# A one-core encoder layer: stages that end without waiting for their last stores, and the Fourier stage's sine unit loaded and folded one stage earlier

## The chip, the cores and the metric

The kernel runs on one core of one Trainium2 chip. The metric is the device time of one execution in microseconds (us); lower is better. The engines are named as in the profile: PE (TensorE, matrix multiplication), PEld (its weight loads), DVE (VectorE), ACT (ScalarE), POOL (GpSimd) and SP (SyncE, which only issues transfers here). SP's transfers go through one hardware queue (q1), POOL's through a software queue (q0), and both are served by the same 16 DMA engines.

## The reference, cut to what matters

Two sequences, of 512 and 2048 tokens with 1024 channels each, go through the same layer. The code works on their 2560 tokens together.

```
x    = layer_norm(x)
proj = x @ w_in                       # 1024 -> 1280: 512 Fourier, 512 q, 128 k, 128 v
f    = real(fft2(u, over tokens and the 128 channels of each of 4 groups)) @ w_fourier
a    = windowed attention (+-128 tokens, ALiBi, sink), 8 query heads, 2 key/value heads
x    = layer_norm(alpha * x + concat(f, a) @ w_out)
h    = square(relu(x @ w_ff1))        # 1024 -> 4096
x    = layer_norm(alpha * x + h @ w_ff2)
```

The answer has to be close to float32, so each large product is three matmuls: both operands are split into a rounded high part and a rest (`split_mm`, lines 65 to 67). ACT makes the high part and DVE the rest.

## The kernel before, in words

The program is six stages, one after the other, each in a block of its own. A block ends for all engines together: the next one starts when every engine, SP among them, has come to the end of its list. Between stages the data lie in DRAM.

- Stage a, `embed_project`: five groups of 512 tokens. In each group DVE normalises, PE transposes, and PE then makes ten units of 128 output rows (`UNITS`): 0 to 3 are queries, 4 keys, 5 values, 6 and 7 the cosine half of the Fourier channels, 8 and 9 the sine half. ACT takes unit m from PSUM into one of four slots of `stage`, and SP stores it to `proj` (line 228); a slot may be filled again when its last store has landed (`stage_st`). DVE also forms sums of the feed-forward weights, which SP loads and stores (lines 192 to 211). In the last group (`more` false) SP loads the DFT tables (line 2272) into what are later the keys' tiles, and, after unit 2, the short sequence's Fourier rows (`load_short_unit`, lines 2266 and 2268). DVE splits three of the five tables and folds the short unit (`fold_short`, line 525).
- Stage b, `fourier`: the transform along the tokens is made of seven units in a fixed order: short, sine0, sine1, left_short, left, cosine0, cosine1. For each, DVE adds or subtracts mirrored halves of the sequence (`fold`, lines 670 and 675), PE transposes the result (`turn`, line 862), ACT and DVE split it (`z_high`, line 767; `z_low`, line 687), and PE multiplies it with the tables in an even part and an odd part (`sums`). Two more tables are split here (`table_high`, line 759; `table_low`, line 681). Then the channel mixing (`mix_short`, `mix_long`) and five stores to `heads` (lines 644 and 649).
- Stage c, `attend`: the attention, 20 blocks of 128 tokens, each stored to `heads` (line 1067).
- Stage d, `mix_out`: the output projection, residual and norm, 20 tiles of 128 tokens. It stores `x1` (line 1378) and, for each pair of tiles, the operands and sums that the next product wants, 1792 KB in `xb` (lines 1382 and 1386).
- Stage u, `mlp_up`: the first feed-forward product in a seven-product scheme. It starts with weight sums that SP loads (line 1627), activations that were loaded during stage d (`x_first`) and four more slices that POOL loads from `xb` at its start (line 1686). Matmuls whose result nobody reads (`keep_busy`, line 73) fill PE's wait at the start of stages c, d, u and e.
- Stage e, `mlp_down`: the second feed-forward product, by far the longest; the change doesn't touch it.

What sets the order around the change: each engine works its own list in order, and waits on semaphores. SP's list holds nearly all transfers, so an SP instruction that waits holds back every transfer behind it. Four stages end with SP waiting for its own last stores: lines 258 and 259 (stage a), 650 and 651 (b), 1069 and 1070 (c), 1387 to 1389 (d).

Of the kernel before, what the change touches and what calls it, by code (L numbers as in the profile page):

```python
# [14 lines left out]
P = 128  # L15
D = 1024
# [88 lines left out]
def embed_project(nc, held, x, ln_g, ln_b, w_in, ident, ident_d, xn_d, proj_d, w2_d, t_d, w1_d, ws_d, k_raw, place, load_mixing,  # L105
                  load_short_unit, load_table, short_parts):
# [6 lines left out]
    with ExitStack() as ctx:  # L113
# [35 lines left out]
        stage_st = al.sems("stage_st", 4)  # L149
# [4 lines left out]
        first_tables, u_short, u_short_ld, t_raw_ld, (half_fold, ends, bias) = short_parts  # L154
        tables_split = al.sem("tables_split")
        PLAIN = FROW - FC

# [10 lines left out]
        def _(sp):  # L168
# [44 lines left out]
            def body(g, more):  # L213
# [3 lines left out]
                if more:  # L217
                    load_quad(g, 0)
                    load_quad(g, 1)
                else:  # L220
                    for i in range(3):
                        load_table(sp, i)
                    load_up(0)
                    load_up(1)
                for m in (1, 0, *range(2, UNITS)):
                    if m:
                        sp.wait_ge(stage_done, g * UNITS + UNITS + m + 1)
                    sp.dma_start(proj_d[m * P:(m + 1) * P, bass.ds(g * GRP, GRP)], stage[:, m % 4, :]
                                 ).then_inc(stage_st[m % 4], 16)
                    if not more and m == 2:  # L230
                        for slot in range(4):
                            sp.wait_ge(stage_st[slot], uses(slot) * 16 + 16)
# [6 lines left out]
                    if more and m in (5, UNITS - 1):  # L239
                        for j in (0, 1) if m == 5 else (2, 3):  # L240
                            store_sums(g, j)
                    if not more and m == 5:
                        store_up(0)
                        store_up(1)
                    if more and m == 5:
                        load_quad(g, 2)
                        load_quad(g, 3)
# [3 lines left out]
            with sp.Fori(0, NG - 1) as g:  # L251
                body(g, True)
# [5 lines left out]
            for s in range(4):  # L258
                sp.wait_ge(stage_st[s], 16 * (uses(s) * NG + 1))
# [32 lines left out]
        def _(dve):  # L292
# [115 lines left out]
            for i, (raw, hi, lo) in enumerate(first_tables):  # L408
# [7 lines left out]
                if i == 1:  # L416
                    dve.wait_ge(u_short_ld, 48)
                    fold_short(dve, u_short, half_fold, ends, bias)

        @block.scalar  # L420
        def _(act):
# [19 lines left out]
            def body(g, first):  # L441
# [12 lines left out]
                for m in range(UNITS):  # L454
                    act.wait_ge(proj_done, g * UNITS + m + 1)
                    act.wait_ge(stage_st[m % 4], g * (16 * uses(m % 4)) + (m // 4) * 16 + 16)
                    is_q = m < KROW // P
                    act.mul(stage[:, m % 4, :], bank[:, m % 8, :], QSCALE if is_q else 1.0
# [6 lines left out]
        def _(pe):  # L465
# [3 lines left out]
            def body(g, first):  # L469
# [17 lines left out]
                for m in range(UNITS):  # L487
                    out = bank[:, m % 8, :]
                    if m >= 8:
                        pe.wait_ge(stage_done, g * UNITS + UNITS + m - 7)  # L490
                    for k in range(KT):
# [4 lines left out]
                        if m == 0:  # L496
# [28 lines left out]
def fold_short(dve, u_short, half_fold, ends, bias):  # L525
# [10 lines left out]
    for kind in range(2):  # L536
        for tiles, op in parts:
            op = op if kind == 0 else {ALU.add: ALU.subtract, ALU.subtract: ALU.add}[op]
            dve.tensor_tensor(to[:, kind, tiles, :], halves[:, 0, tiles, :], halves[:, 1, tiles, :], op)


def fourier(nc, held, proj_d, mixing, ident, u_short, short_table, tables, raw_tables, t_ld, folding, heads_d, load_keys_values,
            load_queries):
# [20 lines left out]
    with ExitStack() as ctx:  # L564
# [5 lines left out]
        heads_more = [al.sb(f"heads{i}", [P, LONG]) for i in range(2)]  # L570
# [6 lines left out]
        mix = al.sb("mix", [P, NFG, 2, P])  # L577
        bank = al.ps("bank", [P, 8, 512])

        u_cos0, u_flat = u_short, u_short.rearrange("p i t -> p (i t)")  # L580
        place = [u_flat, u_a[:], u_b[:], u_left[:, LONG:], u_left[:, 0:LONG], u_flat, u_a[:]]
        out = [heads_more[0][:], heads_more[1][:], u_b[:], u_left[:, 0:LONG], heads_more[0][:]]
# [10 lines left out]
        out_st = al.sems("out_st", 5)  # L593
        block = al.block()

        def folds(n):

            return place[n][:, 0:2 * (ODD0 if units[n] == "left_short" else 512)].rearrange("p (k s) -> p k s", k=2)
# [13 lines left out]
        def _(sp):  # L612
# [17 lines left out]
            load_sines(0, u_a, u_ld[1])  # L630
# [4 lines left out]
            sp.wait_ge(turned, 2 * 0 + 2)  # L635
            sp.dma_start(u_flat, rows(0, P, tok)).then_inc(u_ld[5], 16)
            sp.wait_ge(turned, 2 * 1 + 2)
            sp.dma_start(u_a[:], rows(P, P, tok)).then_inc(u_ld[6], 16)
# [11 lines left out]
            for slot in range(5):  # L650
# [3 lines left out]
        def _(pool):  # L654
            pool.memset(u_left[:], 0.0).then_inc(left_zero, 1)
            pool.memset(y_short[:, :, WIDE0:EVEN0], 0.0).then_inc(y_zero, 1)
            pool.wait_ge(turned, 2 * 5 + 2)
# [4 lines left out]
        def _(dve):  # L662
# [63 lines left out]
            def mirrored_long(g):  # L726
# [3 lines left out]
                if g == 3:  # L730
# [8 lines left out]
            fold(1)  # L739
            z_low(1)  # L740
            table_low(0)
# [14 lines left out]
        def _(act):  # L756
# [12 lines left out]
            def copy_mix():  # L769
                for i in range(2):  # L770
# [51 lines left out]
            def straight_long(g):  # L822
# [3 lines left out]
                if g == 3:  # L826
# [7 lines left out]
            table_high(0)  # L834
            table_high(1)
            z_high(1)
# [16 lines left out]
        def _(pe):  # L853
            def turn(n):
# [3 lines left out]
                for kind in range(2):  # L858
                    if n:
                        pe.wait_ge(fold_done, 2 * (n - 1) + kind + 1)  # L860
# [1540 lines left out]
```

## Time and profile before

| | us |
|---|---|
| median of 3 runs | 2475.83 (2475.64 to 2476.02) |
| the profiled execution's own time | 2474.14 |
| its span | 2472.4 |
| PE busy | 2377.8 (96%) |
| DVE busy | 1578.8 (64%) |
| ACT busy | 1089.9 (44%) |
| DMA moved | 547.76 MB, 222 GB/s |

The span runs from the first to the last recorded instruction; the execution's own time is 1.74 us more. A busy engine is one with an instruction on it; PE's matmuls overlap, so that its busy time is no measure of its peak. Where a row says "[3.50 <-PEq L113]", the engine had been idle for 3.50 us, and what ended that was the event at line 113. PEq, SPq and DVEq are the engines' sequencers, which also carry the block ends; an event of a sequencer at line 113, 564, 967, 1337 or 1564 is the change from one stage to the next.

### The profile page before, as it was taken

The numbers are of one execution on the slowest core, as the hardware profiler recorded it, in microseconds if no ns is written. First come the engines' busy times: TensorE is split into PE (matmuls) and PEld (weight loads), VectorE is DVE, ScalarE is ACT, GpSimd is POOL, SyncE is SP. The second block draws the span as 40 slices with busy tenths as digits, with TensorE's granted clock in tenths as the row PEclk, the third lists the DMA queues.
The fourth block names the chain that finished last, engine by engine and source line by source line (L and its number), as shares of the span: only waits on it lengthen the run. The fifth ranks groups of instructions, "written<-read, shape, count | busy, mean of one in ns | idle before, by whom it ended". The sixth has DMA issues, their size and how long they took to land. (4 is left out here: it accounts for less than half of the span.)

```text
span 2472.4 us, 35019 instructions
## 1 busy us (share of the span) xinstructions
PE 2377.8 (96%) x12038; PEld 2072.4 (84%) x12038; DVE 1578.8 (64%) x2218; ACT 1089.9 (44%) x1770; POOL 181.6 (7%) x245
## 2 busy tenths in 40 slices
PE   6999978999999979999999999999999999999998
PEld 5888866999788858888899989998888888888886
DVE  8644455766566676666766676666455586668667
ACT  3111135888311144444555555555433344444442
POOL 1000001222122210000000000000000010001001
PEclk9999989999999989999999999999999999999999
DMA  7766755223255855555766676668866668777974
GB/s 274 286 270 231 281 164 212 78 72 93 90 196 199 298 238 209 210 214 196 277 240 243 244 278 242 244 230 290 278 195 193 188 216 326 228 219 252 308 226 135
DMA packets 220153, 547.76 MB, mean 222 GB/s; under 512 B 21640, under 2 KB 90888, under 8 KB 200332
## 3 DMA queue, kind: packets, MB, share of 16 engines
q1 hardware_dynamic: 203968, 488.19, 56.8%
q0 software_dynamic: 16080, 58.20, 7.3%
q8 instruction: 62, 1.02, 0.2%
q14 instruction: 43, 0.35, 0.0%
HBM read 365.95 MB, written 180.36 MB: 221 GB/s over the span
## 5 line engine op out<-in xcount | busy, mean ns | idle before, releaser
L65 PE MATMUL e_bank<-e_hi,e_lo 128*128 128x512 f32 x1120 | 435.8, 389 | 0.6 <-DVE e_lo L2112 0.6
L66 PE MATMUL e_bank<-e_lo,e_hi 128*128 128x512 f32 x1120 | 435.7, 389 | 0.0
L67 PE MATMUL e_bank<-e_hi 128*128 128x512 f32 x1120 | 435.7, 389 | 0.0
L65 PE MATMUL u_bank<-u_x_hi,u_wa_lo 128*128 128x384 f32 (+1 forms) x768 | 271.7, 354 | 2.7 <-ACT c_vt_raw L1845 1.4
L67 PE MATMUL u_bank<-u_x_hi,u_wa_hi 128*128 128x384 f32 (+1 forms) x768 | 271.0, 353 | 0.0
L2112 DVE TENSOR_TENSOR e_lo<-e_raw,e_hi 128x896 fp32r<-128x896 f32 (+1 forms) x168 | 189.3, 1134 | 120.6 <-ACT e_hi L2083 119.8
L2083 ACT CAST e_hi<-e_raw 128x896 fp32r<-128x896 f32 (+1 forms) x168 | 165.2, 983 | 209.3 <-PE e_bank L67 199.1
L65 PEld LDWEIGHTS e_bank<-e_hi,e_lo 128*128 128x128 f32 x1120 | 210.2, 188 | 45.1 <-DVE e_lo L2112 1.4
L66 PEld LDWEIGHTS e_bank<-e_lo,e_hi 128*128 128x128 f32 x1120 | 210.2, 188 | 43.7
L67 PEld LDWEIGHTS e_bank<-e_hi 128*128 128x128 f32 x1120 | 210.2, 188 | 43.5
L65 PE MATMUL u_bank<-u_x_hi,u_wb_lo 128*128 128x384 f32 (+1 forms) x576 | 204.9, 356 | 9.2 <-DVE u_x_rest L1694 9.2
L67 PE MATMUL u_bank<-u_x_hi,u_wb_hi 128*128 128x384 f32 (+1 forms) x576 | 204.3, 355 | 0.0
L66 PE MATMUL u_bank<-u_x_rest,u_wb_hi 128*128 128x384 f32 (+1 forms) x576 | 204.3, 355 | 0.0
L66 PE MATMUL u_bank<-u_x_first,u_wa_hi 128*128 128x384 f32 (+1 forms) x576 | 203.4, 353 | 0.0
L65 PEld LDWEIGHTS u_bank<-u_x_hi,u_wa_lo 128*128 128x128 f32 x768 | 144.6, 188 | 15.8 <-issue 2.7
L65 PE MATMUL a_bank<-a_xt_hi,a_w_lo 128*128 128x512 f32 x400 | 156.8, 392 | 0.6 <-DVE a_xt_lo L361 0.6
L66 PE MATMUL a_bank<-a_xt_lo,a_w_hi 128*128 128x512 f32 x400 | 156.2, 391 | 0.0
L67 PE MATMUL a_bank<-a_xt_hi,a_w_hi 128*128 128x512 f32 x400 | 156.1, 390 | 0.0
L67 PEld LDWEIGHTS u_bank<-u_x_hi,u_wa_hi 128*128 128x128 f32 x768 | 144.4, 188 | 10.0
L2112 DVE TENSOR_TENSOR e_lo<-c_q_raw,e_hi 128x896 fp32r<-128x896 f32 (+1 forms) x84 | 94.8, 1134 | 66.8 <-ACT e_hi L2083 66.8
L2112 DVE TENSOR_TENSOR e_lo<-c_vt_raw,e_hi 128x896 fp32r<-128x896 f32 (+1 forms) x84 | 94.9, 1134 | 61.4 <-ACT e_hi L2083 57.9
L1120 DVE CUSTOM_DVE_ANT_0 c_prob<-c_sc,c_bias,c_neg_sink 128x384 f32<-128x384 f32 (+1 forms) x160 | 93.8, 589 | 62.4 <-PE c_sc L1220 44.0
(273 smaller groups left out, 4527.2 us busy)
## 6 DMA issues: line engine op xcount, KB each, us to landing
u_w_sum<-s_ws SPq DMA_DIRECT2D x34, 1024.0 KB, 4.8
c_vt_raw<-w_ff SPq DMA_DIRECT2D x24, 1024.0 KB, 7.8
c_q_raw<-w_ff SPq DMA_DIRECT2D x24, 1024.0 KB, 8.0
s_h<-c_k_raw SPq DMA_DIRECT2D x32, 768.0 KB, 7.2
e_raw<-s_t SPq DMA_DIRECT2D x96, 256.0 KB, 3.7
e_raw<-s_h SPq DMA_DIRECT2D x112, 192.0 KB, 2.8
ab_place<-w_ff SPq DMA_DIRECT2D x18, 1024.0 KB, 8.5
s_h<-c_k_raw SPq DMA_DIRECT2D x96, 192.0 KB, 2.4
```

What stands on the lines that cost most here:

```text
L65: tensor.matmul(out, w_lo, m_hi, start=first, stop=False, skip_group_check=again)
L66: tensor.matmul(out, w_hi, m_lo, start=False, stop=False, skip_group_check=again)
L67: return tensor.matmul(out, w_hi, m_hi, start=False, stop=last, skip_group_check=again)
L1120: dve.tensor_tensor_reduce(prob[:, h % 4, 0:w], sc[:, h % 2, 0:w], bias[:, h, kbs[0] * P:kbs[0] * P + w], 1.0, neg_sink[:, h:h + 1], ALU.a ...
L2083: act.copy(part(hi, n), part(raw, n)).then_inc(hi_done, 1)
L2112: dve.tensor_tensor(part(lo, n), part(raw, n), part(hi, n).bitcast(F32), ALU.subtract).then_inc(split, 1)
```

## The change

Four stages no longer end with the wait for all their last stores. The semaphores of those stores live on into the next stage, and whoever reads the data, or writes over the tile that is being stored, waits there.

The order of the units in stage a changes for every group but the first: 8, 9, 6, 7, 0 to 5. In the last group the short unit is loaded first, ahead of the tables; the sums of `w_ff1` are stored after the fourth unit, tables 3 and 4 are loaded after the fifth and the eighth unit, and after the sixth SP waits for the short unit's fold and loads unit sine0 (`load_sine_unit`), which DVE folds at the end of its list (`fold_sine`). In stage b that fold is gone, and z_high(1) stands ahead of table_high(1), table_low(0) ahead of z_low(1).

```diff
 # embed_project
+        def order(first):
+            sines = FROW // P + 2
+            return list(range(UNITS)) if first else [sines, sines + 1, *range(FROW // P, sines), *range(FROW // P)]
 # SP, last group ahead of the units
+                    load_short_unit(sp)
                     for i in range(3):
                         load_table(sp, i)
                     load_up(0)
                     load_up(1)
-                for m in (1, 0, *range(2, UNITS)):
+                for i in (1, 0, *range(2, UNITS)):
...
-                    if not more and m == 2:
...
-                        load_short_unit(sp)
-                    if not more and m in (6, UNITS - 1):
-                        i = 3 if m == 6 else 4
-                        sp.wait_ge(tables_split, i - 1)
-                        load_table(sp, i)
+                    if not more and i == 3:
+                        store_up(0)
+                        store_up(1)
+                    if not more and i in (4, 7):
+                        table = 3 if i == 4 else 4
+                        sp.wait_ge(tables_split, table - 1)
+                        load_table(sp, table)
+                    if not more and i == 5:
+                        sp.wait_ge(stage_st[0], 16 * (uses(0) * (NG - 1) + 2))
+                        sp.wait_ge(short_folded, 1)
+                        load_sine_unit(sp)
...
-            for s in range(4):
-                sp.wait_ge(stage_st[s], 16 * (uses(s) * NG + 1))
 # DVE, end of the stage
+            dve.wait_ge(u_sine_ld, 64)
+            fold_sine(dve, u_sine, half_fold, sine_folds)
 # new
+def fold_sine(dve, u, half_fold, to):
+    q = SEQS[1][1] // 4
+    low, high = u
+    dve.drain()
+    dve.tensor_tensor(half_fold[:, 0, :], low[:, 1:q + 1], high[:, 2 * q - 1:q - 1:-1], ALU.subtract)
+    dve.tensor_tensor(half_fold[:, 1, :], low[:, 2 * q - 1:q - 1:-1], high[:, 1:q + 1], ALU.subtract)
+    dve.drain()
+    for kind in range(2):
+        dve.tensor_tensor(to[:, kind, :], half_fold[:, 0, :], half_fold[:, 1, :], ALU.add if kind else ALU.subtract)
+        def load_sine_unit(sp):     # 4 transfers of 64 x 1024, 256 KB each
+            for half in range(2):
+                for part in range(2):
+                    tok = SEQS[1][0] + part * 1024
+                    sp.dma_start(u_sine[part][half * HD:(half + 1) * HD, :], ...).then_inc(u_sine_ld, 16)
 # fourier, SP
-            load_sines(0, u_a, u_ld[1])
+            for slot in range(4):
+                sp.wait_ge(stage_st[slot], stores(slot) - 32)
             load_sines(1, u_b, u_ld[2])
...
+            sp.dma_start(u_a[:], rows(P, P, tok)).then_inc(u_ld[6], 16)
+            sp.wait_ge(turned, 2 * 1 + 2)
             sp.dma_start(u_flat, rows(0, P, tok)).then_inc(u_ld[5], 16)
+            for slot in range(4):
+                sp.wait_ge(stage_st[slot], stores(slot))
...
-            for slot in range(5):
+            for slot in range(4):
                 sp.wait_ge(out_st[slot], 16)
 # fourier, POOL ahead of the queries and ACT in copy_mix: wait for stage_st of all slots
 # fourier, DVE and ACT: the order of the first steps
             z_low(0)
-            fold(1)
+            table_low(0)
             z_low(1)
-            table_low(0)
             table_low(1)
...
             z_high(0)
             table_high(0)
+            z_high(1)
             table_high(1)
-            z_high(1)
 # attend, SP
-            for s in range(2):
-                sp.wait_ge(ot_st[s], 16 * (NB // 2))
 # attend: POOL waits for the last Fourier store ahead of load_first_heads, DVE ahead of its first normalise
+            pool.wait_ge(fourier_st, 16)
 # mix_out, SP
-                sp.wait_ge(mixed_st[s], 16 * (NT // 4))
+            sp.wait_ge(mixed_st[0], 16 * (NT // 4))
 # mix_out: POOL ahead of its first load and DVE in norm(0) wait for ot_st of both slots
 # mlp_up, ACT ahead of x_high(0, 2), POOL ahead of the last group
+            act.wait_ge(xb_st, 16 * (NT // 4))
```

Some tiles move, so that what is still being stored isn't written over: `heads_more` behind `mix` (and the last two Fourier outputs into it), `mixed` to the end of `place`, `neg_sink` ahead of `nmax`.

## Rows read from the trace of the kernel before

**Rows 1.** The page: engine's busy time, share of the span, instructions.
```profile
PE 2377.8 (96%) x12038; PEld 2072.4 (84%) x12038; DVE 1578.8 (64%) x2218; ACT 1089.9 (44%) x1770; POOL 181.6 (7%) x245
```
**Rows 2.** PE's waits, whole span: in total, times, longest (us).
```profile
PE u_bank L73 <- PEq L1337: 11.7, 1, 11.7
...
PE b_bank L862 <- PEq L113: 3.5, 1, 3.5
...
PE c_sc L1219 <- DVE c_qs L1112: 1.8, 1, 1.8
```
**Rows 3.** SP's waits, whole span.
```profile
SPq L1389 <- DMA s_xb<-d_place: 5.5, 1, 5.5
...
SPq L651 <- DMA s_heads<-b_heads: 3.4, 1, 3.4
...
SPq L1070 <- DMA s_heads<-c_ot: 1.9, 1, 1.9
...
SPq L259 <- DMA s_proj<-a_stage: 1.3, 1, 1.3
```
**Rows 4.** SP in order of time: start, us, instruction; the stage ends.
```profile
318.84 0.33 SPq L228 DMA_DIRECT2D s_proj<-a_stage  x1
...
321.64 1.18 SPq L621 DMA_DIRECT2D b_u_a<-s_proj  x2
...
400.43 0.33 SPq L649 DMA_DIRECT2D s_heads<-b_u_left  x1
...
408.17 0.34 SPq L1061 DMA_DIRECT2D c_bias<-bias  x1
...
883.69 0.32 SPq L1382 DMA_DIRECT2D s_xb<-d_place  x1
887.71 0.32 SPq L1386 DMA_DIRECT2D s_xb<-d_place  x1
894.03 15.49 SPq L1627 DMA_DIRECT2D u_w_sum<-s_ws  x2
```
**Rows 5.** PE at the one change of stage without such a wait (u to e).
```profile
1696.56 1.95 PE L73 MATMUL e_bank<-c_k_raw 128*128 128x512 f32 x4 [0.30 <-PEq L1564]
```
**Rows 6.** Stage b's start, all engines in order of time.
```profile
324.02 3.81 ACT L759 CAST b_t_last<-c_k_raw 128x2112 fp32r<-128x2112 f32 x2
...
329.82 1.29 DVE L670 TENSOR_TENSOR b_folding<-b_u_a 128x512 f32<-128x512 f32 x2 [4.97 <-DMA b_u_a<-s_proj]
...
332.03 1.94 PE L862 MATMUL b_bank<-ac_ident,b_u_a 128*128 128x128 f32 x8 [5.15 <-DVE b_u_a L675]
...
334.00 0.58 ACT L767 CAST b_z_hi<-b_bank 128x512 fp32r<-128x512 f32 x1 [0.27 <-PE b_bank L862]
...
335.23 4.62 DVE L681 TENSOR_TENSOR b_t_last<-c_k_raw,b_t_last 128x2112 fp32r<-128x2112 f32 x2
```
**Rows 7.** Windows: PE, PEld, DVE, ACT, POOL busy (count), granted clock, DMA.
```profile
321.60:326.90 5.30, 4.64 (x20) 4.08 (x20) 1.38 (x2) 3.94 (x4) 2.31 (x2) 0.52 1.03 300
...
417.70:420.00 2.30, 1.75 (x10) 1.32 (x10) 1.24 (x5) 1.06 (x4) 1.35 (x2) 1.00 1.02 417
```
**Rows 8.** DVE in the last group of stage a.
```profile
301.30 1.43 DVE L532 TENSOR_TENSOR b_folding<-c_q_raw 128x256 f32<-128x256 f32 x4
...
307.44 1.26 DVE L413 CAST b_table<-c_k_raw 128x2112 fp32r<-128x2112 f32 x1 [2.80 <-issue]
```
**Rows 9.** Issues of 269 to 297 us: KB each, median us to landing.
```profile
c_q_raw<-s_proj SPq DMA_DIRECT2D x1, 512.0 KB, 14.8
```
**Rows 10.** Issues of 403 to 420 us, and DVE's first need of the bias.
```profile
c_bias<-bias SPq DMA_DIRECT2D x1, 1536.0 KB, 7.0
...
416.37 1.22 DVE L1112 TENSOR_TENSOR c_qs<-c_q_raw,c_qs 64x1024 fp32r<-64x1024 f32 x1 [0.17 <-issue]
```
**Rows 11.** Stage u's start: ACT's wait for the sums, and the issues of 888 to 925 us.
```profile
898.91 1.05 ACT L1812 CAST u_wa_hi<-u_w_sum 128x1024 fp32r<-128x1024 f32 x1 [0.20 <-DMA u_w_sum<-s_ws]
...
u_x_rest<-s_xb POOLq DMA_DIRECT2D x4, 1024.0 KB, 10.4
```

More of the change, by code:

```diff
@@ L417, in _ @@
                     dve.wait_ge(u_short_ld, 48)
-                    fold_short(dve, u_short, half_fold, ends, bias)
+                    fold_short(dve, u_short, half_fold, ends, bias).then_inc(short_folded, 1)
+            dve.wait_ge(u_sine_ld, 64)
+            fold_sine(dve, u_sine, half_fold, sine_folds)
         @block.scalar
@@ L453, in body @@
                             w_high_rest(k + early)
-                for m in range(UNITS):
-                    act.wait_ge(proj_done, g * UNITS + m + 1)
-                    act.wait_ge(stage_st[m % 4], g * (16 * uses(m % 4)) + (m // 4) * 16 + 16)
+                for i, m in enumerate(order(first)):
+                    act.wait_ge(proj_done, g * UNITS + i + 1)
+                    act.wait_ge(stage_st[i % 4], g * (16 * uses(i % 4)) + (i // 4) * 16 + 16)
                     is_q = m < KROW // P
-                    act.mul(stage[:, m % 4, :], bank[:, m % 8, :], QSCALE if is_q else 1.0
+                    act.mul(stage[:, i % 4, :], bank[:, i % 8, :], QSCALE if is_q else 1.0
                             ).then_inc(stage_done, 1)
@@ L486, in body @@
                         mm.then_inc(turned, 1)
[L487 to L490, printed above, removed]
+                for i, m in enumerate(order(first)):
+                    out = bank[:, i % 8, :]
+                    if i >= 8:
+                        pe.wait_ge(stage_done, g * UNITS + UNITS + i - 7)
                     for k in range(KT):
@@ L649, in _ @@
                 sp.dma_start(heads_d[g * P:(g + 1) * P, tok], out[1 + g]).then_inc(out_st[1 + g], 16)
-            for slot in range(5):
+            for slot in range(4):
                 sp.wait_ge(out_st[slot], 16)
@@ L656, in _ @@
             pool.memset(y_short[:, :, WIDE0:EVEN0], 0.0).then_inc(y_zero, 1)
+            for slot in range(4):
+                pool.wait_ge(stage_st[slot], stores(slot))
             pool.wait_ge(turned, 2 * 5 + 2)
@@ L769, in copy_mix @@
             def copy_mix():
+                for slot in range(4):
+                    act.wait_ge(stage_st[slot], stores(slot))
                 for i in range(2):
@@ L1410, in _ @@
             pool.wait_ge(const_set, 2)
+            for s in range(2):
+                pool.wait_ge(ot_st[s], 16 * (NT // 2))
             for n in range(NT):
@@ L1467, in norm @@
                 dve.wait_ge(mix_done, n + 1)
+                if n == 0:
+                    for slot in range(2):
+                        dve.wait_ge(ot_st[slot], 16 * (NT // 2))
                 dve.wait_ge(xn_ld[s], 16 * (n // 2 + 1))
@@ L1552, in _, with mlp_up @@
             transpose(NT - 1)
[L1555 removed]
+def mlp_up(nc, held, xb_d, w1_d, ws_d, h_d, first, xb_st, h_st, h_sum_st, load_down):
     NP = FF // (2 * P)
```

109 lines of the change are left out of this document (62 added, 47 removed).

## The prediction

> **What bounds the kernel now.** I read the page first: PE has an instruction on it for 96% of the span [rows 1], so time can go only where PE stands still or where its clock is low. Then PE's waits in total: the reader is to see that the longest single ones end in a sequencer event at a change of stage, 11.7 us ahead of stage u and 3.5 ahead of stage b [rows 2], and that others stand inside the start of stage b. Then SP's waits: four of them, 1.3, 3.4, 1.9 and 5.5 us, are the waits for a stage's own last stores [rows 3], and SP in order of time shows that the next stage's first issue follows each at once [rows 4]. So the four ends of stages are bound by the landing of stores, and stage b's start by a load and its fold: PE waits 5.15 us there for the fold of unit sine0 [rows 6]. Nothing else in the change lies on a path that PE waits for.
>
> **What a block end costs by itself.** At the end of stage d SP's last issue ends at 887.71 + 0.32 = 888.03, its wait at 893.53, and the next issue stands at 894.03 [rows 3, 4]: 0.5 us for the change itself. At the one change that has no such wait PE is idle 0.30 us only [rows 5]. I take 0.5 for each.
>
> **1. Stage a to b.** Before, the last store is issued by 319.17, and stage b's SP begins at 321.64 [rows 4]. Between them lie the issue of table 4, the 1.3 us wait and 0.5. After, table 4 is issued earlier in the group and the wait is gone: b begins at 319.17 + 0.5 = 319.7, **1.9 us earlier**. The sine unit's read in b of `stage_st` asks for stores that landed several units before. The cost end: nothing if DVE is done by then, which is the cover to be checked in step 5.
>
> **2. Stage b's start.** The load of sine0 and its fold leave stage b (four DVE instructions, two pairs of 1.29 us), and turn(1) no longer waits for them. What is late next? PE is free for turn(1) at 332.03 - 5.15 = 326.88, thus 325.0 with step 1's shift. From the start of turn(1) to the end of the second z_high it is 334.58 - 332.03 = 2.55 us: 327.5. Now table_high(1) stands behind it, half of 3.81 = 1.9: 329.4. Then table_low(1), half of 4.62 = 2.3: 331.7 [rows 6]. Before, the two table_low ended at 339.85 [rows 6]. Everything of stage b behind that hangs on DVE's order: take_cosines_short, fold(2), turn(2). Its other inputs (u_b, now the first load of the stage; the left rows; the tables) are issued as early or earlier. So **8.1 us** if PE runs as it did, 6.2 of them inside b.
>
> PE's clock adds to it. In 321.6 to 326.9 the granted clock was 0.52, half, after PE's idle time at the change; in 417.7 to 420.0, right behind an idle time of 1.8 us, it was 1.00 [rows 2, 7]. After the change the idle time ahead of stage b falls to 3.5 - 1.9 = 1.6 us, nearest to the second row. At full clock the 4.64 us of PE's work ahead of turn(1) and the turn itself halve; with the latencies between PE, ACT and DVE I count 1.2 us off up to turn(1) and 0.9 in it, **2.1 us** in all, since each ACT step that follows starts that much earlier. I take it, as an estimate from these rows; the ends are 0 and 2.6. Steps 1 and 2: 1.9 + 6.2 + 2.1 = **10.2 us**, ends 8.1 and 10.7.
>
> The added waits in b (POOL ahead of the queries, ACT in copy_mix, SP ahead of the keys) ask for the stores of stage a's last group, issued by 319.17, and are reached 20 us or more later: nothing. The output tiles trade places, and the third output now waits for the short store, more than 10 us old by then: nothing.
>
> **3. Stage b to c.** SP's wait was 3.4 us; it began at 408.17 - 0.5 - 3.4 = 404.27. A store of a group takes 0.33 + 3.4 = 3.7 us; the third group's, issued at 400.43, landed at 404.1 [rows 3, 4]. So without the last one the wait is over when it begins: **3.4 us** off. Against it: the bias (1536 KB) is now issued while that last store still holds the queue. It took 7.0 us to land from 408.17, thus 415.2, and DVE came to it at 416.37 [rows 10]: 1.2 us of cover. The remaining 3.4 us of store less some 1 us of start-up that can overlap takes up to 2.4 of it. Cost between 0 and 1.2, I take 0.2, since the last part of a landing is latency in which the bias already moves. **3.2 us**, ends 2.2 and 3.4.
>
> **4. Stage c to d.** The 1.9 us wait goes [rows 3]. ACT's and DVE's first work there reads what landed in stage c; the loads that need the last stores come 2.9 us into the stage, and the stores are in by then. **1.9 us**, ends 1.6 and 1.9.
>
> **5. Stage d to u.** SP now waits for the last but one `xb` store only. The last took 0.32 + 5.5 = 5.8 us [rows 3, 4]; the one of 883.69 therefore landed at 889.5, and stage u begins at about 890.0 instead of 894.03: 4.0 us earlier. But what paces the start of u is ACT's L1812 at 898.91, which waited for the weight sums, 0.20 us [rows 11]; they landed 4.9 us after their issue. Now the sums (1 MB) are issued on SP's queue behind a store of 1792 KB that lands at 893.5, so that its data end near 892.9. One MB at 417 GB/s, the rate of a full window [rows 7], is 2.5 us, a landing adds about 0.6, and POOL's four loads of 1 MB [rows 11], also 4 us earlier, take a share of the engines from about 894 on, which I put at 1 us. So the sums land at 892.9 + 2.5 + 0.6 + 1.0 = 897.0 against 898.9: **1.9 us**. Ends: 4.0 if the sums were not held at all, and below nothing, -1.8, if POOL's loads take half from their issue on (2.1 MB of SP's queue and as much of POOL's from 890.6 at 417 GB/s is 10.1 us, 900.7). Past this ACT and DVE work back to back until PE's wait for `u_x_rest`, so the shift stays.
> The Trainium skill ("DMA: Bandwidth & Descriptors", Queues, rings and completion order) says that each DMA engine takes turns between the queue rows that have work, a packet at a time. By it the sums share from the moment that POOL's descriptors are there; counted from the issue it would give the end of -1.8 and a total of 13.5 us, which is the rival on the sums below. That the wait of 0.20 us stood so small before is no proof of the rule or against it.
>
> **6. The last group of stage a.** This is what the moved work costs. The short unit (1 MB) now runs ahead of the tables and of `w_ff1`: at 300 to 417 GB/s [rows 7] DVE's sums are 2.5 to 3.5 us later, so fold_short begins at 301.30 + 2.8 = 304.1 [rows 8] and ends 3.3 us later, 307.4. SP stands at its wait for it, with the stores of units 6 to 9 and table 4 behind; ACT needs their slots only at 312.9 and 318.2, PE needs no bank of them: nothing. The sine unit's four issues end near 309.9 (0.59 each [rows 4]). DVE splits table 2 meanwhile, 307.4 to 311.2. Before, sine0 needed 8.2 us from its issue to the fold with a table ahead of it [rows 4, 6]; with table 3 ahead that gives 315.7, and the fold (2.7 us) ends at 318.4. DVE would be done 0.8 us ahead of SP's last issue. Cost 0; each us later costs one.
>
> **Sum.** 10.2 + 3.2 + 1.9 + 1.9 = 17.2 us. The profiled execution took 2474.14, so 2456.9 by its own time; the median of the runs shown is 1.7 us above it. Predicted: **2458.6 us**.
>
> **Rivals.**
> - Clock low at stage b's start. For: so it was in the rows, and in this start PE works in short bursts. Against: the idle time is halved. Total 15.1, 2460.7 us. Chance 0.22.
> - The sums of stage u land late, by taking turns with POOL's loads. For: both queues are served at once. Against: before, both began together as well, and the sums still landed in 4.9 us. Total 17.2 - 1.9 - 1.8 = 13.5, 2462.3 us. Chance 0.12.
> - The waits go but the next stage is held by something else (a code load, the engines' own start), 1 us at each of four changes. Against: the 0.30 us of stage e [rows 5]. 13.2, 2462.6 us. Chance 0.05.
> - The sine unit's fold ends stage a. For: the short unit once took 14.8 us to land [rows 9]; by that from 309.9 the fold ends at 327.4, 8.2 late, total 9.0, 2466.8 us. Against: the queue is nearly empty by 308. Chance 0.04.
> - The other side, slower: the same place, SP's list in order. If the wait for quad sums, table split and short fold grows so that the sine unit's landing comes two such times after its issue, 309.9 + 29.6, the fold ends at 342.2, stage b begins at 342.7 instead of 319.7, and the total is 23.0 - 17.2 = 5.8 us slower, 2481.6. It decides from a fold that ends after 336.4. Chance 0.03.
> - The change doesn't do what it says: a new wait in the readers (ACT ahead of x_high(0, 2), DVE in its first norm) stands for the same landing. Against: each is reached after it by the rows. Within 0.2%, 2474. Chance 0.04.
>
> **How the numbers follow.** The forecast has 0.50. Its own ends: -1.5 (clock partly low), -1.0 (bias), -1.0 (sums), +2.1 (sums not held), so 2456 to 2461.5. The range takes in the first three rivals: 2454.5 to 2464.5. What a measurement can tell from no change is 0.2%, 5 us: faster by more than that holds for the forecast and the first four rivals, 0.93; within it 0.04; slower 0.03.
>
> **What would show it.** After: SP's waits at the four ends gone, or under 0.5 us; PE's idle time ahead of b near 1.6 us; turn(1) right behind the short unit's sums, granted clock 1.00 in b's first 3 us (else the first rival); the two table_low end about 10 us after b's start, against 18; no DMA wait of DVE or PE behind table 2's split at the end of stage a, and DVE done before SP; ACT's L1812 waiting 2 to 3 us for the sums in u. Wrong: PE idle more than 2 us at a change with a DMA behind it, DVE's fold_sine later than SP's last store, or stage c's first bias add later than its matmul.

## The result, and the profile after the change

| | before | after |
|---|---|---|
| median, us | 2475.93 (2475.64 to 2476.51, 4 runs) | 2461.31 (2460.95 to 2461.50, 4 runs) |
| the profiled execution, us | 2474.14 | 2461.47 |
| its span, us | 2472.4 | 2459.8 |
| PE busy, us | 2377.8 | 2373.9 |

The ratio is 0.9943, with a 95% interval of 0.9931 to 0.9954: 14.6 us faster. Forecast were 2458.6 us and 17.2 us off, so some 2.7 us too much. The two profiled executions differ by 12.7 only. The last matmul of stage a starts at 317.80 before and at 319.72 after. In the eleven runs below it stands between 317.58 and 319.60, so this is scatter of stage a (after the change PE's first wait, for a load at the start, took 13.9 us against 12.7, and the granted clock was 0.83 in the first 40 us against 1.00), and the sums are made from stage to stage.

SP's waits for the stores of the stage that ends (in total, times, longest, us). The first is the only one left at a stage's end, where there were four, of 5.5, 3.4, 1.9 and 1.3 us [rows 3]; the second is the new reader's wait at the start of stage b:

```profile
SPq L1423 <- DMA s_xb<-d_place: 1.2, 1, 1.2
...
SPq L650 <- DMA s_proj<-a_stage: 0.2, 1, 0.2
```

PE's waits for a change of stage, and the one for stage c's first queries:

```profile
PE u_bank L73 <- PEq L1372: 7.4, 1, 7.4
PE c_sc L1254 <- DVE c_qs L1145: 4.6, 1, 4.6
...
PE c_pt L1288 <- PEq L588: 1.7, 1, 1.7
PE b_bank L896 <- PEq L113: 1.7, 1, 1.7
PE d_turn L73 <- PEq L1001: 1.5, 1, 1.5
```

They were 11.7 ahead of u and 3.5 ahead of b [rows 2]. The end of stage a and the start of b, in order of time (start, us, instruction), DVE and then PE:

```profile
317.83 0.69 DVE L559 TENSOR_TENSOR b_folding<-c_q_raw,c_vt_raw 128x512 f32<-128x512 f32 x1 [4.46 <-DMA c_vt_raw<-s_proj]
...
319.20 1.29 DVE L563 TENSOR_TENSOR c_q_raw<-b_folding 128x512 f32<-128x512 f32 x2
...
330.31 2.36 DVE L714 TENSOR_TENSOR b_t_last<-c_k_raw,b_t_last 128x2112 fp32r<-128x2112 f32 x1 [1.16 <-ACT b_t_last L791]
```
```profile
319.72 0.39 PE L67 MATMUL a_bank<-a_xt_hi,a_w_hi 128*128 128x512 f32 x1
...
321.84 1.07 PE L896 MATMUL b_bank<-ac_ident,c_q_raw 128*128 128x128 f32 x8 [1.73 <-PEq L113]
...
325.88 1.93 PE L896 MATMUL b_bank<-ac_ident,c_q_raw 128*128 128x128 f32 x8
...
337.81 1.94 PE L896 MATMUL b_bank<-ac_ident,b_u_b 128*128 128x128 f32 x8 [4.09 <-DVE b_u_b L708]
```

The reader is to see that turn(1), at 325.88, waits for nothing (before 5.15 us, [rows 6]), that the second table_low ends at 332.67, 10.8 us behind the stage's start, and that DVE's fold ends stage a at 320.49, behind PE's last matmul but ahead of SP's last issue (321.16). But turn(1) takes 1.93 us, which is its time at half clock; the first turn, with the same eight instructions, took 1.07. Windows of stages b and c (columns as in [rows 7]; the granted clock is the third number from the end):

```profile
321.80:324.50 2.70, 1.70 (x14) 1.49 (x14) 1.29 (x2) 2.00 (x3) 2.19 (x2) 1.00 0.74 216
324.60:327.80 3.20, 3.20 (x18) 3.20 (x17) 2.34 (x2) 1.41 (x2) 0.03 (x1) 0.50 0.93 202
328.00:334.00 6.00, 4.44 (x35) 4.03 (x34) 4.75 (x7) 3.65 (x6) 0.00 (x0) 1.00 0.88 347
356.10:361.40 5.30, 5.30 (x25) 5.30 (x26) 2.21 (x7) 1.36 (x4) 0.00 (x0) 0.50 0.39 162
408.40:412.00 3.60, 3.19 (x12) 2.64 (x13) 1.82 (x8) 1.58 (x6) 1.35 (x2) 0.50 1.03 422
```

TensorE was granted full clock (2.4 GHz) at the start of b, then half (1.2 GHz) for 3.4 us, and half again around the wait of 4.09 us ahead of turn(2) (from 334.8 to 341.6) and where it had just stood still for 3.04 us (at 356) and for 4.56 us (at 408). Stage u's start, SP, ACT and the issue with its landing (KB, median us to landing):

```profile
876.84 0.32 SPq L1420 DMA_DIRECT2D s_xb<-d_place  x1
878.88 0.34 SPq L1666 DMA_DIRECT2D u_w_sum<-s_ws  x1
```
```profile
886.37 1.05 ACT L1853 CAST u_wa_hi<-u_w_sum 128x1024 fp32r<-128x1024 f32 x1 [2.82 <-DMA u_w_sum<-s_ws]
```
```profile
s_xb<-d_place SPq DMA_DIRECT2D x1, 1792.0 KB, 6.9
u_w_sum<-s_ws SPq DMA_DIRECT2D x1, 1024.0 KB, 7.5
```

The sums needed 4.9 us before and ACT waited 0.20 for them [rows 11]. The two traces from piece to piece, all by PE's starts (turn(2) is the MATMUL L896 on b_u_b; "4th wait of u" is the wait of PE for DVE's x_low of 1.14 us that ends at 918.88 before and at 906.37 after):

| piece | before | after | gain | predicted |
|---|---|---|---|---|
| last matmul of a to first of b | 3.88 | 2.12 | 1.8 | 1.9 |
| b's start to turn(2) | 23.30 | 15.97 | 7.3 | 8.3 |
| turn(2) to b's last matmul | 57.08 | 58.40 | -1.3 | 0 |
| b's last to c's first | 6.13 | 2.76 | 3.4 | 3.2 |
| c's first to c's last | 222.75 | 223.09 | -0.3 | 0 |
| c's last to d's first | 4.14 | 2.16 | 2.0 | 1.9 |
| d's last to 4th wait of u | 37.90 | 36.26 | 1.6 | 1.9 |
| sum | | | 14.4 | 17.2 |

### The profile page after: what moved, and what is told of

Same layout as the page of the kernel before. It is cut to its first block and busy times, and to the rows that moved or that the text cites. A ratio compares the mean times of both kernels' runs of the same rounds, so it can differ in the third digit from the quotient of the medians.

```text
span 2459.8 us, 35018 instructions
## 1 busy us (share of the span) xinstructions
PE 2373.9 (97%) x12038; PEld 2071.2 (84%) x12038; DVE 1579.1 (64%) x2218; ACT 1089.4 (44%) x1770; POOL 180.7 (7%) x245
```

## The experiments

Eleven runs, of ten kernels, were made beside the kernel before, on three chips, where its medians were 2475.27, 2475.94 and 2476.72. The theory: the stores' waits and the sine unit's load are worth what the prediction says, and the 2.7 us that are lacking are TensorE's clock (2.6 us in the second, third and fifth rows of the table). Each kernel is the changed one with the edit shown. Medians are compared with the changed kernel's 2461.31, with the ratio to the kernel before of the same chip beside it. From the 4th wait of u to the end, which no edit reaches, the traces took between 1553.4 and 1558.0 us (1553.5 before, 1553.4 after), so a difference of 1 or 2 us is read from the stages and not from the medians.

**The four waits put back** (one of four alike shown):

```diff
             for j in range(TPG):
                 sp.wait_ge(xn_st[j], 16 * (NG + 1))
+            for s in range(4):
+                sp.wait_ge(stage_st[s], 16 * (uses(s) * NG + 1))
```

> The changed kernel with the four waits of SP for a stage's own last stores put back; the sine unit stays in stage a. Theory (the waits stand on the path that PE waits for, each worth what the comparison of the two traces gave: a to b 1.8, b to c 3.4, c to d 2.0, d to u 1.65 us): 8.8 us slower than the changed kernel, so about 2470.1 us, and PE's idle time ahead of stages b and u back at 3.5 and 11.7 us. First rival (another wait, such as the start of the engines or the code, holds the next stage anyway): under 5 us slower, and PE's idle time at the changes grows by less than SP's waits. Second rival (stage b's start is slowed by the clock as well when the idle time ahead of it is 3.5 us): 10 to 11 us slower, with the granted clock at half from b's first instruction.

Measured: 2469.16 us (2467.24 to 2471.18, 9 runs), ratio 0.9971 (0.9961 to 0.9981), 7.8 us slower. PE's waits for a change of stage:

```profile
PE u_bank L73 <- PEq L1376: 11.1, 1, 11.1
PE c_pt L1292 <- PEq L590: 5.2, 1, 5.2
PE d_turn L73 <- PEq L1003: 3.5, 1, 3.5
PE b_bank L898 <- PEq L113: 3.4, 1, 3.4
```

By pieces, against the changed kernel: a to b 1.7 us longer, b to c 3.4, c to d 2.0, d to the 4th wait of u 1.7; that is 8.8, as expected. Stage b inside was 0.5 us quicker and stage c 0.9, which leaves 7.4. At the end of d the wait moved stage u's start by 4.3 us (13.1 us behind the start of d's last matmuls against 8.8), but the time by 1.7 only. In stage c the clock is the likely reason: PE began it at half clock after 5.2 us of idle time, its keep-busy matmuls there took longer, the idle time ahead of the scores was 1.8 us and not 4.56, and the clock was full from 6 us into the stage on; the kernel without any half clock in c, further down, took the same 222.2 us. The first rival falls; of the second only half is true, since half clock at b's start (PE was at half for nearly all of the first 7 us) cost b up to the second table_low 0.7 us against the changed kernel.

**The sine unit back in stage b** (its load and fold taken out of stage a, and into SP's, DVE's and ACT's lists of b where they were):

```diff
-                    if not more and i == 5:
...
-                        load_sine_unit(sp)
...
-            dve.wait_ge(u_sine_ld, 64)
-            fold_sine(dve, u_sine, half_fold, sine_folds)
...
+            load_sines(0, u_a, u_ld[1])
             load_sines(1, u_b, u_ld[2])
...
             z_low(0)
-            table_low(0)
+            fold(1)
             z_low(1)
+            table_low(0)
             table_low(1)
```

> The changed kernel with the sine unit's load and fold put back into stage b (SP, DVE and ACT orders of stage b as before); no stage waits for its last stores. Theory (the move is worth what the two traces show from stage b's start to the end of the second table_low, 7.3 us, and the last group of stage a gives nothing back): 7.3 us slower than the changed kernel, about 2468.6 us. The granted clock may move it: if PE's idle time of 5 us ahead of turn(1) is what let the clock drop later in stage b, the 1.3 us that the changed kernel lost behind turn(2) come back, and it is 6.0 us slower, 2467.3. Rival (the fold in stage a pushes that stage's end out): stage a ends earlier than in the changed kernel by over 0.5 us, and the sum is under 6 us slower for that reason.

Measured: 2467.96 us (2465.29 to 2469.10, 6 runs), ratio 0.9967 (0.9955 to 0.9979), 6.6 us slower. PE at stage b's start:

```profile
320.10 1.06 PE L891 MATMUL b_bank<-ac_ident,c_q_raw 128*128 128x128 f32 x8 [1.74 <-PEq L113]
...
330.03 1.94 PE L891 MATMUL b_bank<-ac_ident,b_u_a 128*128 128x128 f32 x8 [5.07 <-DVE b_u_a L702]
...
342.98 1.94 PE L891 MATMUL b_bank<-ac_ident,b_u_b 128*128 128x128 f32 x8 [3.54 <-DVE b_u_b L702]
```

The wait of 5.1 us is back, and turn(2) is 22.88 us behind the stage's start, 6.9 later than in the changed kernel. From the last matmul of a to the first of b it is 2.12 us, the same as with the fold in stage a: the fold costs stage a nothing. Behind turn(2) stage b took 57.69 us (58.40), so 0.7 of the 1.3 us came back. The rival falls.

**The sine unit's load 2 stores later in stage a** (behind table 4):

```diff
-                    if not more and i == 5:
+                    if not more and i == 7:
                         sp.wait_ge(stage_st[0], 16 * (uses(0) * (NG - 1) + 2))
```

> The changed kernel with the sine unit's load issued behind table 4 in stage a's last group, some 4.2 us later than now. In the changed kernel DVE ended its fold 0.7 us ahead of SP's last issue. Theory (that is the whole cover, and each us beyond it costs one): the fold ends 4 to 5.5 us later, and stage b begins 3.5 to 5 us later than now against the last matmul of stage a (now 2.1 us behind it), so 3.5 to 5.5 us slower than the changed kernel, 2465 to 2467 us. Rival (the queue is nearly empty by then, so the unit lands sooner after its issue, in 4 us as against 8): the fold ends 0 to 1 us later, and the time is within 0.5 us of the changed kernel.

Measured: 2466.64 us (2465.68 to 2468.45, 5 runs), ratio 0.9964 (0.9951 to 0.9978), 5.3 us slower. DVE and PE:

```profile
321.79 0.69 DVE L559 TENSOR_TENSOR b_folding<-c_q_raw,c_vt_raw 128x512 f32<-128x512 f32 x1 [10.62 <-DMA c_vt_raw<-s_proj]
...
323.16 1.29 DVE L563 TENSOR_TENSOR c_q_raw<-b_folding 128x512 f32<-128x512 f32 x2
```
```profile
324.76 1.94 PE L896 MATMUL b_bank<-ac_ident,c_q_raw 128*128 128x128 f32 x8 [6.75 <-PEq L113]
```

Against PE's last matmul (317.62 here) the fold ends 6.8 us later; in the changed kernel it was 0.8. So it moved by 6.1 us, and stage b's start by 7.14 - 2.12 = 5.0: the cover is 1.0 us, and each us beyond it costs one. Behind its longer idle time stage b also ran at half clock for its first 13.4 us, and turn(2) came 17.04 us after the stage's start, 1.1 later than in the changed kernel; that cost was not in the expectation.

**PE kept busy in its idle time** (results that nobody reads):

```diff
             turn(0)
+            keep_busy(pe, bank[:, 3, 0:P], ident[:], ident[:], 5)
             for n in range(N):
+                if n == 4:
+                    keep_busy(pe, bank[:, 7, :], tables[0][0][:, 0:P], tables[0][0][:, 0:512], 12)
                 sums(n, 0)
...
-            keep_busy(pe, tr[:].rearrange("p i t -> p (i t)"), ident[:], vt_raw[:, 0:512], 3)
+            keep_busy(pe, tr[:].rearrange("p i t -> p (i t)"), ident[:], vt_raw[:, 0:512], 7)
```

> The changed kernel with matmuls whose results nobody reads put into PE's idle time: 5 of 128x128 between turn(0) and the short sums in stage b, 12 of 128x512 (fp32r) ahead of the sums of unit 4 in stage b, and 7 instead of 3 (f32, 128x512) ahead of stage c's scores. Theory (of the 2.7 us that the prediction had too much, all is PE's granted clock, 1.0 us at stage b's start, 1.3 us behind the 3 us wait in stage b, 0.4 us at stage c's start, and the clock falls because PE stood still just before): the clock stays at full in the three places and the kernel is 2.0 to 2.7 us faster than the changed one, about 2458.9 us. Rival A (the clock's phase does not follow PE's idle time here): the granted clock falls at about the same instants, and the kernel is 0 to 1 us slower, since the added matmuls end later at half clock than the wait they fill. Rival B: only the longest idle time (stage b's middle) matters, 1.3 us faster.

Measured: 2457.70 us (2456.41 to 2458.51, 5 runs), ratio 0.9926 (0.9912 to 0.9939), 3.6 us faster than the changed kernel. To turn(2) 14.59 us (15.97), from there to b's last matmul 56.36 (58.40), stage c 222.96 (223.09): 1.4 + 2.0 + 0.1. That is more than the 2.0 to 2.7 expected, since b's start gained more than it had lost. In two of the three places the clock stayed at full; in stage c, where 1.1 us of idle time were left, it still fell, for 4 us. Rival A falls, and so does B. Around the wait ahead of turn(2) the clock was still at half.

**More of it**, 16 in the wait ahead of turn(2), 8 in stage c:

```diff
                 sums(n, 0)
+                if n == 1:
+                    pe.wait_ge(z_split, 2 * n + 2)
+                    keep_busy(pe, bank[:, 0, :], tables[0][0][:, 0:P], tables[0][0][:, 0:512], 16)
                 if n + 1 < N:
                     turn(n + 1)
```

> The kernel with the added matmuls in stage b and c (2457.7 us), with 16 more of 128x512 (fp32r) in PE's 4.1 us of idle time ahead of turn(2), and 8 instead of 7 ahead of stage c's scores. Theory (the clock falls to half behind idle time, and it was at half from 13 to 20 us after stage b's start in every run, behind this wait or inside it): no half clock is left in stage b, turn(2) and the 16 turns of the mixing matrices run at full, and the kernel is 1.0 to 1.7 us faster than the one with fewer, about 2456.3 us. Rival (that stretch is bound by DVE and ACT, not by PE): the clock is full but the time is the same within 0.4 us; or the added matmuls, at 0.23 us each, run past the end of the wait and cost up to 0.5 us.

Measured: 2455.17 us (2453.81 to 2456.21, 5 runs), ratio 0.9917 (0.9903 to 0.9930). This is the fastest kernel of the study, 6.1 us below the changed one. Windows of stages b (the first five) and c:

```profile
319.70:322.40 2.70, 2.69 (x24) 2.66 (x24) 1.29 (x2) 2.02 (x3) 2.21 (x2) 1.00 0.77 225
322.50:325.70 3.20, 2.99 (x28) 2.85 (x26) 2.36 (x2) 2.71 (x4) 0.01 (x1) 1.00 0.89 197
325.90:331.90 6.00, 5.13 (x33) 4.59 (x34) 5.88 (x11) 2.19 (x5) 0.00 (x0) 1.00 0.90 346
350.00:354.00 4.00, 3.74 (x29) 3.31 (x28) 2.98 (x8) 2.18 (x7) 0.00 (x0) 1.00 0.72 288
354.00:360.00 6.00, 5.20 (x33) 4.32 (x32) 1.29 (x2) 5.39 (x9) 2.82 (x4) 1.00 0.52 128
404.00:408.00 4.00, 3.29 (x27) 2.93 (x25) 3.25 (x11) 3.37 (x14) 0.00 (x0) 1.00 1.04 316
```

No half clock was left in b or c. From turn(2) to b's last matmul it took 53.96 us, less than before the change (57.08), and stage c 222.23. What lies behind the wait of 3.04 us can be laid side by side over all traces: b's last matmul came 39.9 to 40.2 us after that wait in the four executions that had 5.5 to 6.1 us of half clock there (the changed kernel among them), 38.7 to 39.0 in the four with 2.8 to 3.8 (the kernel before among them), and 37.4 to 37.5 in the five with PE kept busy, without half clock.

**The changed kernel and this one once more**, on one chip:

> The changed kernel once more, beside the two below. In three kernels with the same instructions in the first 12 us of stage b the granted clock fell to half after 2.8 us for 3.2 us (the changed kernel), after 2.7 us for 10 (sums on POOL's queue) and not at all (POOL's loads held), and the second table_low ended 10.8, 11.1 and 9.4 us after the stage's start. Theory (the clock there changes from one execution to the next, since PE's idle times of 1 us stand close to what it takes): its median is within 1 us of 2461.3, and the second table_low ends 9.4 to 11.1 us after the stage's start. Rival (the difference belongs to the kernel as built): 10.8 again.

> The kernel with all the added matmuls in stages b and c, beside the changed kernel on the same chip. Theory: with PE busy in its idle times the clock stays at full through stage b in this execution too, and it is 5 to 7 us faster than the changed kernel, about 2455.2 us. Rival (the full clock of the last run was chance): half clock of 3 us or more somewhere in stage b, and 2457 to 2460 us.

Measured: 2461.83 (2458.27 to 2462.53, 5 runs), ratio 0.9936 (0.9922 to 0.9949), and 2456.29 (2454.97 to 2458.45, 5 runs), ratio 0.9917 (0.9903 to 0.9931): 5.5 us apart. The changed kernel's second execution at stage b's start:

```profile
320.00:322.00 2.00, 1.06 (x8) 0.86 (x8) 0.67 (x2) 1.28 (x3) 1.47 (x1) 1.00 0.57 199
322.60:331.80 9.20, 9.20 (x45) 9.20 (x45) 6.41 (x7) 5.44 (x8) 0.24 (x2) 0.50 0.94 279
```

The clock was at half for 10 us this time, where the first execution had 3.4. Four executions with the same instructions there, and five with PE kept busy:

| kernel | half clock in b's first 13 us | second table_low ends | turn(2) |
|---|---|---|---|
| changed | 3.4 | 10.8 | 15.97 |
| changed, again | 10 | 11.5 | 16.59 |
| sums on POOL's queue (below) | 10 | 11.1 | 16.22 |
| POOL's loads held (below) | none | 9.4 | 14.58 |
| PE kept busy, five executions of four kernels | none | 9.4 to 9.5 | 14.58 to 14.60 |

So the clock after the change is not one value but differs between executions, and moves turn(2) by up to 2.0 us; with PE busy it is the same each time. The second table_low ended at 11.5, a little outside the 9.4 to 11.1 that was expected, and the rival (10.8 again) falls. The reason that the theory gave in brackets, the idle times of 1 us, is borne out in so far as the five executions in which matmuls fill one of them had no half clock; how short an idle time has to be, no run shows. The busy kernel had no half clock in b again, so its rival falls too.

**Stage u's sums on POOL's queue**, ahead of POOL's four loads:

```diff
         @block.gpsimd
         def _(pool):
+            pool.dma_start(w_sum[:], ws_d[0:P, :].rearrange("p (b c) -> p b c", b=4)).then_inc(w_sum_first, 16)
...
-            load_w_sums(0)
```

> The changed kernel with the first weight sums of stage u loaded by POOL's queue, ahead of its four loads, and not by SP's queue behind the last store of xb. Theory (the sums land 7.5 us after their issue because they stand behind that store on their queue): they land about 5 us after their issue, ACT's wait of 2.8 us for them falls under 0.5 us, and the kernel is 1.5 to 2.5 us faster than the changed one, about 2459.3 us. Rival (store, sums and POOL's loads share the DMA engines, and the queue makes no difference): the sums land within 0.5 us of where they did, the rest of x lands later, and the kernel is 0 to 1 us slower.

Measured: 2461.68 us (2461.20 to 2462.66, 5 runs), ratio 0.9944 (0.9930 to 0.9958), no gain. ACT came to the sums at 885.42, 8.1 us behind PE's first matmul of u (7.4 before the edit), 7.4 us after their issue. The theory fell: taking the sums out from behind the store on SP's queue did not bring them sooner.

**POOL's loads held until the sums are in:**

```diff
                     if g:
                         pool.wait_ge(prod_done, (g * NP - 1) * NPROD + j + 1)
+                    elif j == NFIRST:
+                        pool.wait_ge(w_sum_ld, 16)
```

> The changed kernel with POOL's four loads of the rest of x in stage u held until the first weight sums have landed. With the sums on POOL's queue they still landed 8.1 us after the stage's start against 7.4, so the store of xb ahead of them on SP's queue is not what held them. Theory (the bytes of POOL's loads take the DMA engines' time from the store and the sums: from 877.9 to 886.4 us the engines moved some 3.5 MB, of which store and sums are 2.9): the sums land 1.0 to 1.6 us earlier, ACT's wait of 2.8 us falls to 1.2 to 1.8, the rest of x still lands before ACT comes to it 11.7 us into the stage, and the kernel is 1.0 to 1.6 us faster than the changed one, about 2460.0 us. Rival A (the landing is latency of the chain store, semaphore, load, and no share): the sums land where they did and the rest of x lands 4 us later, 0 to 3 us slower. Rival B (the sums gain, but x's last tile comes late): PE shows a DMA-bound wait 15 to 25 us into the stage, and the time is within 0.5 us of the changed kernel.

> Both of the above: all the added matmuls, and POOL's loads in stage u held until the sums have landed. The two act in different stages, so by the theories their gains add: 4.9 + 1.3 us off the changed kernel's 2461.3, about 2455.1 us. If only the matmuls help: 2456.4. If holding the loads costs: 2457 to 2459.

Measured: 2462.62 us (2459.11 to 2464.61, 5 runs), ratio 0.9947 (0.9933 to 0.9960), no gain; with the busy PE 2457.25 (2455.21 to 2458.73, 5 runs), ratio 0.9924 (0.9911 to 0.9938), which is 2.1 above the one without. ACT in u:

```profile
884.44 1.05 ACT L1855 CAST u_wa_hi<-u_w_sum 128x1024 fp32r<-128x1024 f32 x1 [2.57 <-DMA u_w_sum<-s_ws]
...
890.34 1.90 ACT L1842 CAST u_x_hi<-u_x_rest 128x2048 fp32r<-128x2048 f32 x1 [1.58 <-DMA u_x_rest<-s_xb]
```

The sums came 0.25 us sooner and the rest of x so late that PE's 4th wait ends 1.4 us later. So POOL's loads take 0.25 us from the sums, not the 1.0 to 1.6 of the theory. Rival A holds but for its reason, latency: by the bytes of each queue, SP's queue in this run moves 1.26 MB in the first 3 us of stage u, which are the store's, and then the sums' 1 MB, with POOL's queue empty. In the changed kernel it is the same, and POOL's first bytes come in the seventh us only.

**The sums in two halves** (on top of the busy PE):

```diff
-            load_w_sums(0)
+            for half, loaded in ((0, w_sum_half), (1, w_sum_ld)):
+                sp.dma_start(w_sum[:, 2 * half:2 * half + 2, :], ...).then_inc(loaded, 16)
```

> The kernel with all the added matmuls, and in stage u the first weight sums loaded as two halves of 512 KB, with ACT waiting for the first half ahead of its first cast of them and for the second ahead of the next. Theory (the sums come when the store's bytes and their own have passed the DMA engines, at 417 GB/s): the first half lands 1.2 us earlier, ACT's wait falls from 2.8 to 1.6 us, and the kernel is 0.5 to 1.2 us faster than the one without the split, about 2454.2 us. Rival A (what follows is held by the rest of x, which lands when it did): the wait falls but reappears ahead of x's fourth tile, no gain. Rival B (two transfers of one queue run side by side and end together): the first half lands no earlier, no gain.

Measured: 2458.54 us (2456.32 to 2458.95, 5 runs), ratio 0.9925 (0.9912 to 0.9939), 2.3 us slower than the kernel without the split on the same chip. PE began u at 870.85; ACT:

```profile
877.69 1.05 ACT L1861 CAST u_wa_hi<-u_w_sum 128x1024 fp32r<-128x1024 f32 x1 [2.21 <-DMA u_w_sum<-s_ws]
...
882.32 1.05 ACT L1868 CAST u_wb_hi<-u_w_sum 128x1024 fp32r<-128x1024 f32 x1 [1.79 <-DMA u_w_sum<-s_ws]
```

The first half was there after 6.8 us, 0.6 sooner than the whole, and the second after 11.5. By the bytes of each queue the second half moved in the eighth to eleventh us of the stage, 0.52 MB beside 1.08 MB of POOL's, while the whole had been through by the seventh. PE's 4th wait ended 1.9 us later than without the split; PE had stood still for 3.14 us before that, and its clock was at half for the 3 us behind. The theory fell, and neither rival had this outcome.

## Why the prediction was right, and where it was off, step by step

The time lies in the range, and the gains came from the waits and the load that the prediction named. The median is at the edge of the forecast's own ends (2456 to 2461.5), and nearer to the first rival's 2460.7 than to the forecast. That nearness is partly luck: the rival had the clock low all through b's start, while it was low for part of it, and more than half of what was lacking lay in places that no sum had.

- **Step 1, a to b: 1.9 forecast, 1.8 found,** and 1.7 when the wait was put back.
- **Step 2, the load and the fold (6.2): right.** The run with the later sine load had half clock for b's first 13.4 us, as the kernel before had (13.5), and turn(2) at 17.04: 23.30 - 17.04 = 6.3 us are the load and the fold alone. With full clock the gain up to turn(2) is 23.30 - 14.59 = 8.7 us; 6.2 + 2.1 were forecast. The order of what is late next (z_high, table_high(1), table_low(1)) is the one in the trace.
- **Step 2, the clock (2.1): the mis-sized term.** "After the change the idle time ahead of stage b falls to ... 1.6 us, nearest to the second row. At full clock the 4.64 us of PE's work ahead of turn(1) and the turn itself halve." The idle time did fall to 1.73 us and the clock was at full in b's first 2.7 us, but at half in turn(1): in the four executions the term brought 1.1, 0.5, 0.9 and 2.5 us (in the order of the table above; 23.30 less turn(2)'s place, less 6.2). The first rival was this one (0 instead of 2.1), and what happened lies between.
- **Behind turn(2): taken as 0, found -1.3.** All that lies behind was assumed to move along as it was. The wait of 3.04 us for ACT was the same in both kernels, but the half clock behind it lasted 6.1 us after the change and 2.8 before, and from that wait to b's last matmul it took 40.15 us against 38.70. It goes away with matmuls in that wait. The changed kernel again took 58.17 from turn(2) on, the sine unit back in b 57.69, the four waits back 57.16.
- **Step 3, b to c: 3.2 forecast, 3.4 found.** The bias took 8.0 us to land, as against 7.0 [rows 10], and used up the cover of 1.2 us, but cost nothing here: DVE came to it 8.15 us after PE's start of stage c, 8.18 before, and the 0.17 us of idle time stood there before as well. In the changed kernel's second execution the same wait was 0.76 us, so the 0.2 charged is the right size. DVE's first need of it:

```profile
407.12 1.22 DVE L1145 TENSOR_TENSOR c_qs<-c_q_raw,c_qs 64x1024 fp32r<-64x1024 f32 x1 [0.17 <-DMA c_bias<-bias]
```
 But in stage c the keep-busy matmuls that stood there already now run at full clock and end 4.6 us ahead of the scores, where they had ended 1.8 ahead [rows 2]; the clock falls in that gap. Cost 0.3 us against the kernel before (0.9 against the same stage at full clock behind the scores), not in the prediction.
- **Step 4, c to d: 1.9 forecast, 2.0 found.**
- **Step 5, d to u: 1.9 forecast, 1.6 found, the size right and one part of the reason wrong.** SP waits 1.2 us, as step 5 implies (the list of signs, with "under 0.5 us", does not fit it), the stage starts 4.3 us earlier, and the sums take it back: 7.4 us from the stage's start, against 4.9 with the wait put back. The prediction had them behind the store "on SP's queue" and then 1.0 us of sharing with POOL. The store's share is in the traces: SP's queue is busy with its last 1.3 MB for the first 3 us of the stage, and the sums' bytes come behind. The sharing was 0.25 us, since POOL's bytes come too late to matter. Whether it has to be the same queue stays open. With the sums on POOL's queue the store again took the first 3 us and the sums' bytes came behind it, but before the change too, with no store under way, POOL's first bytes came in the fifth us only, so that queue may have been late by itself. No run took the store away alone. The Trainium skill ("DMA: Bandwidth & Descriptors", Queues, rings and completion order) has the engines take turns between queues; the rival built on that gave 13.5 us in total by counting the sharing from the issue, and for this load the trace does not bear its size out: 0.25 us, not 3.7.
- **Step 6, the last group of a: cost 0 forecast, 0 found.** The fold ended at 320.49 for 318.4 forecast, with the profile's stage a 1.9 us later, so 318.6 in the frame of before; the cover of 0.8 us is 1.0 by experiment.

Of the 2.7 us, 1.0 are the clock at b's start, 1.3 behind turn(2), 0.3 in c: 2.6 of PE's clock. For b the runs show this; for c it rests on comparing traces. Keeping PE busy brought back 3.6, and where it stood in the last wait as well, 6.1.

## What to carry to other kernels

A wait for a stage's own last stores can cost its whole length if the next stage does not read them (three of the four did, 7.1 us by the run that put them back; the fourth and longest cost 1.7 of 4.3 us): let the reader wait, and check by the bytes what the first load of the next stage now stands behind. When an edit shortens or moves PE's idle times, price the clock behind every idle time that follows, not the first alone; here a few unread matmuls in waits of 1 to 4 us that PE had anyway made that price vanish, and were worth about 40% of what the change itself brought (6.1 and 5.5 us). A transfer that is moved up has a cover that can be measured by moving it back until it costs.

## What the runs showed of the hardware

- The granted clock at one and the same place differed between executions of the same instructions: in stage b's first 13 us half clock for 0, 3.4, 10 and 10 us. So a single profile of this kernel does not show what the clock will be there.
- The same 1 MB needed 4.9 us to land in an empty stretch and 7.5 behind a store of 1792 KB, on the store's queue; on another queue it needed 7.4, where that queue's own late start may have had a part.
- 1 MB in one transfer landed after 7.4 us of stage u, in two of 512 KB after 6.8 and 11.5. The second half moved beside POOL's loads, 0.52 MB of it against 1.08 MB of theirs in the same 4 us; why it had not begun before them is open.
